# Expert stage: the first half of the next expert's rows is transposed ahead of the second half of gate and up

## The chip, the cores and the metric

One core of one Trainium2 chip runs the whole program. The metric is the device time of one execution in microseconds (us). Before the change it is 2176.31 us, the median of 3 runs (2172.53 to 2176.81).

The core's engines work side by side and meet at semaphores: TensorE (PE, and PEld for its weight loads), VectorE (DVE), ScalarE (ACT), GpSimd (POOL), which here issues the indirect transfers and small copies, and SyncE (SP), which issues the other transfers. Each engine runs its own instructions in the order in which they are written.

## The reference, cut to what matters

One layer of a decoder over 2048 prompt tokens and 64 sample tokens: a mixer (attention beside a short convolution), then 64 routed experts, of which each token uses 6, and one shared expert. The change lies in the routed experts:

```python
def step(acc, blk):
    tok, g, e = blk
    xb = xpad[tok]                                        # rows of the block's tokens, 1024 wide
    hid = jax.nn.silu(xb @ w_gate[e]) * (xb @ w_up[e])    # 1024 -> 256, twice
    yb = (hid @ w_down[e]) * g[:, None]                   # 256 -> 1024
    return acc.at[tok].add(yb.astype(acc.dtype)), None
```

## The kernel before

The program has four stages: mixer, dense part (output projection, norm, router, shared expert), routed experts (`stage_experts`, from about 1000 us of the span on), and the last norm. Only the third is changed.

All products are made from two parts for precision: an operand is rounded to a high part (by ACT) and the rest is taken as the low part (by DVE). "Round" and "split" below are these two steps, for weights (`round_w`, L1707; `split_w`, L1804) and for rows (`round_x`, L1714; `split_x`, L1809).

An expert takes up to n rows: 256 for the first two, then 176, 192, 208, 224, 240 and 256 in six classes (`CLASSES`, L61) with 10, 14, 10, 12, 8 and 8 experts. Experts go in pairs p; b is the place in the pair, and expert e = 2p + b. Rows come as two halves t, of 128 and of n - 128 rows. What each engine does for an expert:

- POOL gathers the rows into `xg` (L1663), one indirect transfer for each half, and later adds the outputs into memory (L1646).
- PE transposes a half with 8 instructions of 128x128 into `psX` (L1867). There is one `psX`, so the second half must wait until ACT and DVE have read the first (`s_xl`, L1865).
- ACT rounds that half into `xs` (L1714), and DVE splits it (L1809). There is one `xs` (beyond the first pair), so the rounding of expert e's first half must wait until both halves of gate and up of expert e-1 are done (`s_gu`, L1713).
- PE computes gate and up in two halves f of 128 of the 256 hidden columns (`gate_up`, L1870): 32 matmuls each, in turn of 2n columns (L1881) and of n columns (L1883), into `psU`. When one f is done, ACT first copies its second part out (`copy_lo`, L1686), DVE adds (L1786), then come a sigmoid (L1691) and products.
- PE computes down of expert e-2, for each half t 12 matmuls of 512 columns into `psY` (L1859 to L1861), and ACT writes the scaled output (L1724).

In one step of PE, which this text numbers by the expert e whose rows are transposed, stand: gate and up of e-1 with f = 1, transpose of e's first half, down of e-2 for its first half, transpose of e's second half, down of e-2 for its second half, gate and up of e with f = 0. The order of ACT is written out by hand in its own `pair` (L1743) and that of DVE likewise (L1828): on ACT, `copy_lo(e-1, 1)` stands directly ahead of `round_x` of e's first half. The first pair (`fresh`) has another order. So 62 of the 64 experts, e = 2 to 63, have the step above.

The lines that make the waits named in the prediction:

```python
pe.wait_ge(s_row[2 * b + t], 16 * (p + 1))             # L1864: rows gathered
after(pe, s_xl, 2 * e + t - (1 if fresh(p) else 0))    # L1865: psX read by the split
act.wait_ge(s_xT, 2 * e + t + 1)                       # L1711: transposed
after(act, s_gu, 2 * e)                                # L1713: gate and up of e-1 done
```

Of the kernel before, what the change touches and what calls it, by code (L numbers as in the profile page):

```python
# [140 lines left out]
def after(eng, sem, count):  # L141


    if not (isinstance(count, int) and count <= 0):
        eng.wait_ge(sem, count)
# [1383 lines left out]
def stage_experts(nc, io, ov, raw, ent, s_ent, s_w, s_norm):  # L1529
    PAIRS = NE // 2  # L1530
    with ExitStack() as ctx:
# [48 lines left out]
        def pairs(eng, pair, peeled=1):  # L1580


            pair(0, BLK, BLK, None)
            more = eng.value_load(ov[0:1, MORE:MORE + 1], min_val=0, max_val=OVP)
            before = BLK
            for begin, end, n in CLASSES:
                for p in range(begin, begin + peeled):
                    pair(p, before, n, None)
                    before = n
                with eng.Fori(begin + peeled, end) as p:  # L1590
                    pair(p, n, n, None)
            with eng.If(more > 0):
                with eng.Fori(0, OVP) as j:
                    with eng.If(more > j):
                        pair(PAIRS + j, BLK, BLK, j)
            return PAIRS + more
# [257 lines left out]
        @block.tensor  # L1854
        def _(pe):
            pe.wait_ge(s_const, 16)

            def three(out, lh, ll, rh, rl, start, stop):
                nc.tensor.matmul(out, lh, rh, start=start, stop=False)  # L1859
                nc.tensor.matmul(out, lh, rl, start=False, stop=False)  # L1860
                return nc.tensor.matmul(out, ll, rh, start=False, stop=stop)  # L1861

            def transpose_x(p, e, b, t):
                pe.wait_ge(s_row[2 * b + t], 16 * (p + 1))  # L1864
                after(pe, s_xl, 2 * e + t - (1 if fresh(p) else 0))  # L1865
                for kc in range(KC):
                    last = nc.tensor.transpose(rows_T(p, t)[:, kc * P:(kc + 1) * P], xg[:, 2 * b + t, kc * P:(kc + 1) * P], ident[:])  # L1867
                last.then_inc(s_xT, 1)

            def gate_up(e, b, f, n):  # L1870
                if not exists(e):
                    return
                if f == 0:
                    pe.wait_ge(s_xl, 2 * e + 2)
                after(pe, s_sum, 2 * e + f - 1)
                for half in range(2):
                    c0 = half * FF + f * P
                    for kc in range(KC):
                        if f == 0 and half == 0 and kc % 2 == 0:
                            pe.wait_ge(s_split, 6 * e + kc // 2 + 1)  # L1880
                        nc.tensor.matmul(psU[:, f, half, 0:2 * n].rearrange("p (s n) -> p s n", s=2), guh[:, b, kc, c0:c0 + P],  # L1881
                                         rows_split(e)[:, kc, :, 0:n], start=(kc == 0), stop=False)
                        last = nc.tensor.matmul(psU[:, f, half, 0:n], gul[:, b, kc, c0:c0 + P], rows_split(e)[:, kc, 0, 0:n],  # L1883
                                                start=False, stop=(kc == KC - 1))
                last.then_inc(s_gu, 1)

            def down(e, b, t, n):
                if not exists(e):
                    return
                pe.wait_ge(s_hl, 2 * e + 2)  # L1890
                pe.wait_ge(s_split, 6 * e + 6)
                r = rows_of(n, t)
                for half in range(2):
                    u = 2 * t + half
                    after(pe, s_y, 4 * e + u - 1)
                    for f in range(FC):
                        last = three(psY[0:r, half, :], hdh[:, b, f, t * P:t * P + r], hdl[:, b, f, t * P:t * P + r],
                                     dnh[:, b, f, half * 512:(half + 1) * 512], dnl[:, b, f, half * 512:(half + 1) * 512],
                                     f == 0, f == FC - 1)
                    last.then_inc(s_dn, 1)  # L1900

            def pair(p, n1, n, j):
                for b in range(2):
                    e = 2 * p + b
                    if not fresh(p):
                        gate_up(e - 1, 1 - b, 1, n if b else n1)
                    for t in range(2):
                        transpose_x(p, e, b, t)
                        down(e - 2, b, t, n1)
                    if fresh(p):  # L1910
                        gate_up(e - 1, 1 - b, 1, n)
                    gate_up(e, b, 0, n)

            e = 2 * pairs(pe, pair)
            for t in range(2):
                down(e - 2, 0, t, BLK)
            gate_up(e - 1, 1, 1, BLK)
            pe.wait_ge(s_split, 6 * e)
            pe.wait_ge(s_y, 4 * e - 4)
            pe.wait_ge(s_sum, 2 * e - 1)  # L1920
            for f in range(FC):
                pe.wait_ge(s_hl, 2 * e - 1 + f)
                for u in range(4):
                    t, half = u // 2, u % 2
                    last = three(last_sums(u), hdh[:, 1, f, t * P:(t + 1) * P], hdl[:, 1, f, t * P:(t + 1) * P],
                                 dnh[:, 1, f, half * 512:(half + 1) * 512], dnl[:, 1, f, half * 512:(half + 1) * 512],
                                 f == 0, f == FC - 1)
                    if f == FC - 1:
                        last.then_inc(s_dn, 1)
# [197 lines left out]
```

## Time and profile before

| | value |
|---|---|
| median of 3 runs | 2176.31 us (2172.53 to 2176.81) |
| the profiled execution | 2175.58 us, span 2173.8 us |
| PE busy | 2056.9 us, 95% of the span |
| DVE busy | 1429.4 us, 66% |
| ACT busy | 1208.0 us, 56% |
| POOL busy | 573.5 us, 26% |
| mean granted TensorE clock | 0.976 of full speed |
| memory traffic | read 316.91 MB, written 98.12 MB |

The profiled execution is 0.73 us shorter than the median of the runs. Its span is the time from the first to the last recorded instruction, and 1.8 us of the execution lie around it. A busy share is a mean over all stages. PE's matmuls overlap in the records: a matmul of 512 columns is recorded with 0.39 us, while the next one starts 0.23 us after it. So the distance from start to start tells what a matmul costs, not its recorded length.

### The profile page before, as it was taken

Reading aid. Unit: us, or ns where it says so; the run is one execution under the profiler, and the core shown is the slowest. Engines: PE = TensorE matmul, PEld = TensorE weight load, DVE = VectorE, ACT = ScalarE, POOL = GpSimd, SP = SyncE. Lnnn points to the kernel's source line nnn. Section 1 sums busy time; section 2 is a strip of 40 time slices with the busy share of each in tenths; the row PEclk is TensorE's granted clock in tenths of the full one; section 3 lists DMA queues with packets and bytes.
Section 4 is the critical chain, followed back from the end, with each engine's and each line's share of the span. In section 5 each row is a group of like instructions: output and inputs, shape, how many; then the busy total and the mean of one; then the engine's idle time right before and its main releaser. Section 6 shows DMA issues by size and latency. Waiting matters only on the chain. (4 is left out here: it accounts for less than half of the span.)

```text
span 2173.8 us, 36506 instructions
## 1 busy us (share of the span) xinstructions
PE 2056.9 (95%) x11572; PEld 1739.6 (80%) x11572; DVE 1429.4 (66%) x2742; ACT 1208.0 (56%) x2133; POOL 573.5 (26%) x659
## 2 busy tenths in 40 slices
PE   7999999999899999986999999999999999999970
PEld 5787777777678888875988889989988888888860
DVE  6444454444668787876777777777777777777738
ACT  5343443443533333323777777777777777767648
POOL 1111111111112323233233333333333333333320
PEclk9999999999999999998999999999999999999985
DMA  6111011010453223246799999999999999999957
GB/s 213 49 42 38 30 37 44 30 36 34 164 202 102 92 93 101 83 172 217 223 307 271 293 297 277 293 299 283 277 290 293 292 293 286 290 287 286 285 111 302
DMA packets 113290, 413.81 MB, mean 190 GB/s; under 512 B 35185, under 2 KB 39793, under 8 KB 85521
## 3 DMA queue, kind: packets, MB, share of 16 engines
q1 hardware_dynamic: 75344, 290.02, 36.1%
q0 software_dynamic: 37872, 122.90, 25.1%
q8 instruction: 36, 0.59, 0.1%
q14 instruction: 38, 0.30, 0.0%
HBM read 316.91 MB, written 98.12 MB: 191 GB/s over the span
## 5 line engine op out<-in xcount | busy, mean ns | idle before, releaser
L1881 PE MATMUL ex_psU<-ex_xs,ex_guh 128*128 128x384 f32 (+5 forms) x2016 | 620.6, 371 | 2.4 <-DVE ex_xs L1809 2.4
L1883 PE MATMUL ex_psU<-ex_xs,ex_gul 128*128 128x192 f32 (+5 forms) x2016 | 523.0, 259 | 0.0
L1881 PEld LDWEIGHTS ex_psU<-ex_xs,ex_guh 128*128 128x128 f32 x2016 | 378.6, 188 | 34.3 <-DVE ex_xs L1809 2.6
L1883 PEld LDWEIGHTS ex_psU<-ex_xs,ex_gul 128*128 128x128 f32 x2016 | 384.4, 191 | 2.5
L1646 POOL DMA_INDIRECT acc_d<-ex_y,ex_rows x128 | 198.9, 1554 | 397.4 <-ACT ex_y L1724 380.7
L1663 POOL DMA_INDIRECT ex_xg<-h_d,entries x128 | 143.8, 1124 | 345.7 <-issue 214.9
L1859 PE MATMUL ex_psY<-ex_dnh,ex_hdh 128*128 128x512 f32 x508 | 209.6, 413 | 1.9 <-DVE ex_hdl L1798 1.0
L1861 PE MATMUL ex_psY<-ex_dnh,ex_hdl 128*128 128x512 f32 x508 | 200.0, 394 | 0.0
L1860 PE MATMUL ex_psY<-ex_dnl,ex_hdh 128*128 128x512 f32 x508 | 199.0, 392 | 0.0
L1724 ACT ACTIVATE ex_y<-ex_psY,ex_use 128x512 f32<-128x512 f32 x254 | 169.4, 681 | 27.5 <-PE ex_psY L1861 27.1
L1786 DVE TENSOR_TENSOR ex_gu<-ex_psU,ex_lo 128x384 f32<-128x384 f32 (+5 forms) x128 | 77.3, 604 | 151.3 <-ACT ex_lo L1686 150.0
L1809 DVE TENSOR_TENSOR ex_xs<-ex_psX,ex_xs 128x512 fp32r<-128x512 f32 (+5 forms) x125 | 130.7, 1046 | 61.7 <-ACT ex_xs L1714 56.7
L717 PE MATMUL mi_psG<-mi_gh,mi_xh 128*128 128x512 f32 x408 | 168.7, 414 | 0.9 <-DVE mi_gl L539 0.9
L1804 DVE TENSOR_TENSOR ex_gul<-mi_g_raw,ex_guh 128x1024 fp32r<-128x1024 f32 x128 | 155.9, 1220 | 10.1 <-ACT ex_guh L1707 10.1
L1804 DVE TENSOR_TENSOR ex_gul<-mi_g_place,ex_guh 128x1024 fp32r<-128x1024 f32 x128 | 155.9, 1220 | 8.5 <-ACT ex_guh L1707 8.5
L717 PE MATMUL mi_psG<-mi_gl,mi_xh 128*128 128x512 f32 x408 | 160.4, 393 | 0.0
L717 PE MATMUL mi_psG<-mi_gh,mi_xl 128*128 128x512 f32 x408 | 160.4, 393 | 0.0
L1686 ACT ACTIVATE ex_lo<-ex_psU 128x384 f32<-128x384 f32 (+5 forms) x128 | 67.1, 524 | 159.1 <-PE ex_psU L1883 158.1
L1707 ACT ACTIVATE ex_guh<-mi_g_raw 128x1024 fp32r<-128x1024 f32 x128 | 134.1, 1050 | 11.2 <-PEq L895 11.2
L1867 PE MATMUL ex_psX<-ex_ident,ex_xg 128*128 128x128 f32 x1008 | 131.4, 273 | 7.0 <-DMA ex_xg<-h_d,entries 7.0
L1707 ACT ACTIVATE ex_guh<-mi_g_place 128x1024 fp32r<-128x1024 f32 x128 | 134.0, 1050 | 0.0
L1867 PEld LDWEIGHTS ex_psX<-ex_ident,ex_xg 128*128 128x128 f32 x1008 | 115.9, 141 | 16.1 <-issue 7.1
(398 smaller groups left out, 4180.8 us busy)
## 6 DMA issues: line engine op xcount, KB each, us to landing
mi_g_raw<-w_experts SPq DMA_DIRECT2D x96, 1024.0 KB
mi_g_place<-w_experts SPq DMA_DIRECT2D x96, 1024.0 KB
mi_xr<-xT SPq DMA_DIRECT2D x17, 512.0 KB, 3.7
acc_d<-de_acc SPq DMA_DIRECT2D x17, 512.0 KB, 13.3
h_d<-de_h POOLq DMA_DIRECT2D x17, 512.0 KB
de_cr<-cat SPq DMA_DIRECT2D x16, 512.0 KB
de_xr<-x_rows SPq DMA_DIRECT2D x16, 512.0 KB
mi_g_raw<-w_conv SPq DMA_DIRECT2D x6, 1024.0 KB, 20.9
```

Source lines behind the costliest of these rows:

```text
L717: last = nc.tensor.matmul(psG[:, (k + j) % 2, :], a[:, k, kc, :], b[:, j, kc, :], start=(kc == 0 and n == 0), stop=(kc == KC - 1 and n == 2))
L1646: nc.gpsimd.indirect_dma_start(out=io["acc_d"], out_offset=bass.IndirectOffsetOnAxis(ap=rows[0:r, 2 * b + t:2 * b + t + 1].bitcast(U32), a ...
L1663: nc.gpsimd.indirect_dma_start(out=xg[0:r, k, :], out_offset=None, in_=io["h_d"], in_offset=bass.IndirectOffsetOnAxis(ap=ent[0:r, k, 0:1]. ...
L1707: A(hi, src, ACT.Copy).then_inc(s_round, 1)
L1724: A(y[0:r, k, half * 512:(half + 1) * 512], sums(u)[0:r], ACT.Copy, scale=use[0:r, k, 1:2].bitcast(F32)).then_inc(s_y, 1)
L1804: V.tensor_tensor(lo, src, hi.bitcast(F32), ALU.subtract).then_inc(s_split, 1)
L1859: nc.tensor.matmul(out, lh, rh, start=start, stop=False)
L1860: nc.tensor.matmul(out, lh, rl, start=False, stop=False)
L1861: return nc.tensor.matmul(out, ll, rh, start=False, stop=stop)
L1867: last = nc.tensor.transpose(rows_T(p, t)[:, kc * P:(kc + 1) * P], xg[:, 2 * b + t, kc * P:(kc + 1) * P], ident[:])
L1881: nc.tensor.matmul(psU[:, f, half, 0:2 * n].rearrange("p (s n) -> p s n", s=2), guh[:, b, kc, c0:c0 + P], rows_split(e)[:, kc, :, 0:n], st ...
L1883: last = nc.tensor.matmul(psU[:, f, half, 0:n], gul[:, b, kc, c0:c0 + P], rows_split(e)[:, kc, 0, 0:n], start=False, stop=(kc == KC - 1))
```

## The change

In the pair of PE, the transpose of the first half (t = 0) is issued ahead of gate and up of e-1 with f = 1, where it stood behind it. The second half's transpose keeps its place between the two parts of down. In the first pair nothing moves, since gate and up is not issued there ahead of the transposes. No instruction of another engine is moved.

```diff
             def pair(p, n1, n, j):
                 for b in range(2):
                     e = 2 * p + b
+                    transpose_x(p, e, b, 0)
                     if not fresh(p):
                         gate_up(e - 1, 1 - b, 1, n if b else n1)
-                    for t in range(2):
-                        transpose_x(p, e, b, t)
-                        down(e - 2, b, t, n1)
+                    down(e - 2, b, 0, n1)
+                    transpose_x(p, e, b, 1)
+                    down(e - 2, b, 1, n1)
                     if fresh(p):
                         gate_up(e - 1, 1 - b, 1, n)
                     gate_up(e, b, 0, n)
```

On PE, between gate and up of expert 2 with f = 0 (176 rows) and the same with f = 1, in the step of expert 3 (`ex_xg` holds the gathered rows, `ex_psX` their transpose, `ex_rows2` says that the first half has been gathered, `ex_xT_lo` that the rows before have been split):

```order
 L1881 MATMUL ex_psU<-ex_xs,ex_guh 128x352
 L1883 MATMUL ex_psU<-ex_xs,ex_gul 128x176
+L1867 MATMUL ex_psX<-ex_ident,ex_xg 128x128 [waits ex_xT_lo,ex_rows2]
+L1867 MATMUL ex_psX<-ex_ident,ex_xg 128x128 x7
 L1881 MATMUL ex_psU<-ex_xs,ex_guh 128x352 [waits ex_summed]
 L1883 MATMUL ex_psU<-ex_xs,ex_gul 128x176
```

The eight transposes of the first half, with their two waits, now stand between the halves of gate and up.

On PE, at the end of the second half of gate and up in the same step, 32 matmuls later, where down of expert 1 begins:

```order
 L1881 MATMUL ex_psU<-ex_xs,ex_guh 128x352
 L1883 MATMUL ex_psU<-ex_xs,ex_gul 128x176
-L1867 MATMUL ex_psX<-ex_ident,ex_xg 128x128 [waits ex_xT_lo,ex_rows2]
-L1867 MATMUL ex_psX<-ex_ident,ex_xg 128x128 x7
 L1859 MATMUL ex_psY<-ex_dnh,ex_hdh 128x512 [waits ex_y,ex_split,ex_hid_lo]
 L1860 MATMUL ex_psY<-ex_dnl,ex_hdh 128x512
```

Down follows gate and up directly, and between the end of gate and up and the transpose of the second half only the 12 matmuls of down are left.

On ACT, in a step of the class of 192 rows, in both kernels alike (`ex_lo` is the target of `copy_lo`, `ex_xs` the rounded rows):

```order
L1686 ACTIVATE ex_lo<-ex_psU 128x2x192 [waits ex_hid,ex_gate_up]
L1714 ACTIVATE ex_xs<-ex_psX 128x8x128 [waits ex_gate_up,ex_xT]
L1691 ACTIVATE ex_lo<-ex_gu 128x192 [waits ex_summed]
L1707 ACTIVATE ex_guh<-mi_g_place 128x1024 [waits gate_up_back_loaded1]
L1724 ACTIVATE ex_y<-ex_psY,ex_use 128x512 [waits ex_added,ex_entries_kept,ex_down]
```

The copy of `psU` stands ahead of the rounding of the first half, and both wait for gate and up; nothing here is moved.

## Rows read from the trace of the kernel before

**Rows 1.** Stretches: time, busy us (count) by engine, clock, DMA share, GB/s.

```profile
1000.00:1030.00 30.00, 21.13 (x114) 18.47 (x114) 22.04 (x24) 17.84 (x22) 11.31 (x11) 0.78 0.85 289
1500.00:1600.00 100.00, 100.00 (x619) 90.95 (x618) 72.11 (x96) 72.10 (x107) 33.09 (x36) 1.00 0.97 287
```

**Rows 2.** Timeline of PE, one step of 208 rows: start us, length us, instruction.

```profile
1501.18 0.35 PE L1881 MATMUL ex_psU<-ex_xs,ex_guh 128*128 128x416 f32 x1
...
1510.66 0.26 PE L1883 MATMUL ex_psU<-ex_xs,ex_gul 128*128 128x208 f32 x1
1510.76 1.03 PE L1867 MATMUL ex_psX<-ex_ident,ex_xg 128*128 128x128 f32 x8
1511.55 0.47 PE L1859 MATMUL ex_psY<-ex_dnh,ex_hdh 128*128 128x512 f32 x1
1511.86 0.40 PE L1860 MATMUL ex_psY<-ex_dnl,ex_hdh 128*128 128x512 f32 x1
...
1514.17 0.40 PE L1861 MATMUL ex_psY<-ex_dnh,ex_hdl 128*128 128x512 f32 x1
1514.41 1.04 PE L1867 MATMUL ex_psX<-ex_ident,ex_xg 128*128 128x128 f32 x8
...
1518.08 0.35 PE L1881 MATMUL ex_psU<-ex_xs,ex_guh 128*128 128x416 f32 x1
```

**Rows 3.** Timeline of ACT in the same step.

```profile
1510.96 0.52 ACT L1686 ACTIVATE ex_lo<-ex_psU 128x416 f32<-128x416 f32 x1
1511.83 1.03 ACT L1714 ACTIVATE ex_xs<-ex_psX 128x1024 fp32r<-128x1024 f32 x1 [0.36 <-issue]
...
1515.48 0.71 ACT L1714 ACTIVATE ex_xs<-ex_psX 128x640 fp32r<-128x640 f32 x1 [0.18 <-PE ex_psX L1867]
```

**Rows 4.** Timeline of DVE in the same step.

```profile
1512.89 1.23 DVE L1809 TENSOR_TENSOR ex_xs<-ex_psX,ex_xs 128x1024 fp32r<-128x1024 f32 x1 [0.79 <-ACT ex_xs L1714]
...
1516.22 0.82 DVE L1809 TENSOR_TENSOR ex_xs<-ex_psX,ex_xs 128x640 fp32r<-128x640 f32 x1 [0.23 <-ACT ex_xs L1714]
```

**Rows 5.** Timeline of PE's weight loads: second half's transposes, same step.

```profile
1514.17 1.03 PEld L1867 LDWEIGHTS ex_psX<-ex_ident,ex_xg 128*128 128x128 f32 x8
```

**Rows 6.** Timelines of PEld and PE: such a load in a later step.

```profile
1598.73 0.96 PEld L1867 LDWEIGHTS ex_psX<-ex_ident,ex_xg 128*128 128x128 f32 x8
1598.90 1.03 PE L1867 MATMUL ex_psX<-ex_ident,ex_xg 128*128 128x128 f32 x8
```

**Rows 7.** Timeline of ACT: the copy, with 256 rows its follower, with 176 alone.

```profile
2032.29 0.60 ACT L1686 ACTIVATE ex_lo<-ex_psU 128x512 f32<-128x512 f32 x1 [3.04 <-PE ex_psU L1883]
2032.79 1.05 ACT L1707 ACTIVATE ex_guh<-mi_g_place 128x1024 fp32r<-128x1024 f32 x1
...
1161.36 0.47 ACT L1686 ACTIVATE ex_lo<-ex_psU 128x352 f32<-128x352 f32 x1 [1.72 <-PE ex_psU L1883]
```

**Rows 8.** Timelines of DVE and PEld in the first expert: a released wait.

```profile
1011.13 1.23 DVE L1809 TENSOR_TENSOR ex_xs<-ex_psY,ex_xs 128x1024 fp32r<-128x1024 f32 x1 [0.84 <-ACT ex_xs L1714]
1012.41 0.19 PEld L1881 LDWEIGHTS ex_psU<-ex_xs,ex_guh 128*128 128x128 f32 x1 [2.61 <-DVE ex_xs L1809]
1012.52 0.19 PEld L1883 LDWEIGHTS ex_psU<-ex_xs,ex_gul 128*128 128x128 f32 x1
```

**Rows 9.** Timeline of PE in the first pair: gate and up behind a transpose.

```profile
1021.36 0.48 PE L1881 MATMUL ex_psU<-ex_xs,ex_guh 128*128 128x512 f32 x1
1021.67 0.28 PE L1883 MATMUL ex_psU<-ex_xs,ex_gul 128*128 128x256 f32 x1
```

**Rows 10.** Timeline of POOL: two gathers for the next expert and an add.

```profile
1510.79 1.15 POOL L1663 DMA_INDIRECT ex_xg<-h_d,entries  x1 [5.26 <-issue]
1512.25 0.93 POOL L1663 DMA_INDIRECT ex_xg<-h_d,entries  x1 [0.30 <-issue]
...
1516.15 1.60 POOL L1646 DMA_INDIRECT acc_d<-ex_y,ex_rows  x1 [2.78 <-ACT ex_y L1724]
```

**Rows 11.** POOL's DMA queue from 1515 to 1520 us: packets, MB, share.

```profile
q0 software_dynamic: 236, 0.87, 57.7%
```

## The prediction

> **What bounds the kernel now.** I read the table of stretches first. In the routed experts PE is recorded busy for all of 100 us, at the full clock of 2.4 GHz (granted 1.00), while DVE and ACT are busy for 72 us each [rows 1]. Only the first 30 us of the stage are different (PE 21.13 us busy, clock 0.78). Since a recorded busy PE can hide small gaps, I then read PE's timeline of one step, from start to start. Gate and up of two halves takes 1510.76 - 1501.18 = 9.58 us, 4.79 us a half. The first half's transposes run from 1510.76; the second matmul of down starts at 1511.86, and from there to the last at 1514.17 are ten matmuls, 0.231 us each. The second half's transposes follow at 1514.41, 0.24 us behind the last matmul of down, which is the same distance as between matmuls of down. So PE has no gap at all [rows 2]. A step costs what PE's instructions cost, and 62 steps stand in a row. Whatever PE waits in a step is added to the time 62 times, and only a wait of PE that exists today could be won.
>
> Next I followed what releases the second half's transposes, because that wait is close. The chain runs over three engines. Gate and up ends at 1510.66 + 0.26 = 1510.92. ACT starts its copy of `psU` at 1510.96, then idles 0.36 us until the transposes are done, and rounds from 1511.83 to 1512.86 [rows 3]. DVE splits from 1512.89 to 1514.12 [rows 4]. The weight load of the second half's first transpose starts at 1514.17 [rows 5], 0.05 us behind the split. The reader is to see that this chain ends just in time: down's last matmul also starts at 1514.17.
>
> **The change, part by part.** PE's instructions are the same in number and kind. The moved piece is eight transposes with two waits and their signal; it issues no DMA and no queue is passed.
>
> What it moves on PE: eight transposes take from 1510.76 to 1511.55 by their starts, and then one load lies bare, since the first two matmuls of down are 0.31 us apart instead of 0.23. That is 0.79 + 0.08 = 0.87 us [rows 2]. Ahead of gate and up they cost the same: where this order exists today, in the first pair, the first two matmuls are also 0.31 us apart [rows 9], with the same 512 columns. So on PE alone the move is worth nothing; I take 0, with 0.05 us a step to either side (3 us in all) for widths that the rows don't show behind a transpose.
>
> What it does to the chain: counted from the end of gate and up, down now starts 0.87 us earlier, and so the second half's transposes are due 0.87 us earlier. Does the rounding start as much earlier? Before, it started 1511.83 - 1510.92 = 0.91 us after gate and up, because it waited for the transposes, and the copy of `psU` lay hidden under them. Now the transposes are long done, but the copy still stands ahead of the rounding on ACT and can't start before gate and up has ended. The rounding starts 0.04 us + one copy after it. A copy costs ACT, from start to start, 0.50 us with 256 rows, that is its recorded 0.60 us less 0.10. With 176 rows it is recorded with 0.47 us, which gives about 0.37 [rows 7]; with 208 rows 0.52 - 0.10 = 0.42 [rows 3]. So the rounding moves up by 0.91 - 0.04 - 0.42 = 0.45 us where 0.87 is needed. Measured against down, the chain ends one copy later than today: 0.42 us with 208 rows.
>
> How much of this is covered? The load starts today 0.24 us ahead of its transpose (1514.17 and 1514.41). In a later step it starts only 1598.90 - 1598.73 = 0.17 us ahead, and nothing follows late, so at least 0.07 us is free [rows 6]. A load that has been released is followed by the next one 0.11 us later (1012.41 and 1012.52), which I take as the time that a bare load needs [rows 8]. So it can come 0.24 - 0.11 = 0.13 us later free of charge. The lower bound of the cover is 0, if 0.07 is luck of the recording; the upper one is 0.24 us, if only the transposes and not their loads waited. I take 0.13, the value nearest to a row.
>
> The sum: the copy by class is 0.37, 0.39, 0.42, 0.45, 0.47 and 0.50 us (evenly from 176 to 256 rows), for 10, 14, 10, 12, 8 and 8 experts: 3.7 + 5.5 + 4.2 + 5.4 + 3.8 + 4.0 = 26.6 us. Less 62 x 0.13 = 8.1 us this is 18.5 us of new waits of PE, 0.24 to 0.37 us each. With cover 0.24 it is 26.6 - 14.9 = 11.7 us, with none 26.6 us.
>
> The bound of 0.24 is also where a rule of the Trainium skill would lead ("TensorE: Matmul & The Clock Gate", Part 2, the step on LDWEIGHTS): PE pulls a weight load ahead of matmuls in flight. By it the loads would be in the array when the wait ends, and the sum would be 11.7 us. The rows show the load itself starting 0.05 us behind the split, both here and in the first expert [rows 4, 5, 8], so I keep 18.5 us.
>
> What is late next: behind PE's new wait, down of the second half, gate and up of the next expert and everything after shift with it, so no second wait arises there. On ACT the second half's rounding idles 0.18 us today for its transposes [rows 3]; ACT falls behind PE by the covered 0.13 us only, so 0.05 us is left. DVE's second split idles 0.23 us [rows 4]. With the full cover of 0.24 us these would cost some hundredths back. ACT's other work gets 0.87 us more ahead of the end of gate and up and 0.87 less behind it, where it idles over 1.7 us before the next copy [rows 7].
>
> What the earlier transposes take away from the gather: the next expert's first transposes would start at 1518.08 + 4.79 = 1522.87 instead of 1527.66. The gathers are issued at 1510.79 and 1512.25 [rows 10]. From 1515 to 1520 POOL's queue moves 0.87 MB [rows 11]; the two gathers are 208 rows of 4 KB, 0.85 MB, and the add behind them is issued only at 1516.15. If the queue is in order, both halves are there by 1520, and the first one, 0.52 MB, sooner: some 3 us to spare. I take 0; not hidden it is a rival below.
>
> **The sum against its own time.** The profiled execution took 2175.58 us (span 2173.8 and 1.8 around it), so 2194.1 us. The median of the runs is 0.73 us above it, which gives 2194.8. I predict 2194.5 us.
>
> **Rivals.**
> - *The chain isn't what PE waits for, and the kernel gets a little faster.* If ACT got through the copy sooner, or if today's transposes are themselves held back by the split, the shorter distance wins something. Place: PE at L1867 of the second half. It decides at a copy of 0.13 us or less, or a cover above 0.42. Price: at most the 0.05 us a step taken above for the seams, 62 x 0.05 = 3 us, so 2172.5 us. Against it: all rows of copies are 0.47 us or longer. With a cover between the two it ends within 4 us of before, about 2178.
> - *The gather comes late.* If the adds share the queue's turns with the gathers, a first half may land only when the burst ends, 2 us behind 1522.87 in my step. For it: DMA is busy at 0.97 [rows 1]. Price: 1 us in a step gives 62 us, 2256 us. Against it: the order and the 3 us to spare.
> - *The clock falls.* Each step now has a gap of PE. In the first 30 us of the stage, with PE 21.13 us busy, the granted clock was 0.78 [rows 1], that is for part of the time at the lower level of 1.2 GHz. Were it 0.97 over 1050 us, this would add 1050 x 0.03 = 32 us: 2226 us. Against it: there PE idled for 9 us of 30, here for 0.3 of 17. The Trainium skill has a rule that speaks for this rival ("TensorE: Matmul & The Clock Gate", "A second HAM failure mode: psum-queue depth-cycling"): frequent short idles between groups of matmuls make the clock swing. No row of this stage shows short idles, so the trace can't settle it; the 0.78 belongs to long ones.
>
> **How the numbers follow.** The forecast gets 0.84, the kernel ending faster 0.04, the cover that is large enough for no change 0.05, the gather 0.03, the clock 0.04. The bounds 11.7 and 26.6 us, with 3 us for the seams at either end, go from 2184 to 2206; the outer ends need both extremes, so the range is 2185 to 2204. What lies outside is mainly the rivals, 0.16. What can be told from no change here is 0.2%, 4.4 us: faster 0.04, same 0.05, slower 0.91.
>
> **What would show it.** In the profile after, PE's waits have a new line, `psX` on DVE's split (L1809), about 62 times with 0.2 to 0.4 us, or, where the profile counts it as busy, the distance from down's last matmul to the second half's transposes grows from 0.24 to about 0.5 us. The step of 208 rows grows from 16.90 by 0.29 us. ACT's copy is followed by the rounding with no idle time between. If the copy and the rounding follow each other and the distance stays at 0.24, the cover was mis-sized. A line of PE waiting for the gather, or a clock below 1.00 between 1100 and 2000 us, would show a rival. If the step is no longer than 16.90 us, the prediction is wrong.

## The result and the profile after

The changed kernel takes 2190.66 us, the median of 4 runs (2187.11 to 2191.82); the kernel before took 2176.56 us beside it (4 runs, 2172.53 to 2177.27). The ratio is 1.0067 with a 95% interval of 1.0055 to 1.0078: slower by 14.1 us. A second set of runs (below) gave 1.0077 [1.0063, 1.0091]. The forecast was 2194.5 us with 2185 to 2204. The profiled execution took 2187.11 us, with a span of 2185.3. One execution each in experiments 2, 8 and 9, and one of the kernel before beside 8 and 9, took 2322 to 7534 us, and the ratios leave these out.

First the page: the busy time of each engine over the span.

```profile
PE 2069.8 (95%) x11572; PEld 1737.7 (80%) x11572; DVE 1428.3 (65%) x2742; ACT 1200.3 (55%) x2133; POOL 576.7 (26%) x659
```

DVE's and ACT's work has not grown, but PE is recorded 12.9 us busier (2056.9 before) with the same instructions. The new time is hidden in PE's busy records.

PE's waits in the expert stage (engine, tile and line, what was waited for: us in total, times, longest us):

```profile
PE ex_psX L1867 <- DMA ex_xg<-h_d,entries: 7.1, 1, 7.1
...
PE ex_psX L1867 <- DVE ex_xs L1809: 0.9, 5, 0.2
```

The second line is new. It has 5 waits and 0.9 us, far below the whole loss, because a matmul that is still recorded as busy covers most of each wait. The first, the gather, is there once, as it was before; no step of the changed order waits for rows.

The row of the weight loads (PEld) shows what PE's row hides. Its waits for these transposes from 1020 to 2100 us:

```profile
PEld ex_psX L1867 <- DVE ex_xs L1809: 22.3, 50, 0.6
PEld ex_psX L1867 <- issue: 6.2, 12, 0.6
```

In the kernel before, neither line is there. So the load now waits in 62 places, which is the number of steps, and for 50 of them the split is named as what released it. The 28.5 us are idle time of the load row, not the loss: part of them is covered by matmuls that still run.

The stretches of [rows 1], with one more near the end of the stage (time, busy us and count by engine PE, PEld, DVE, ACT, POOL, then clock, DMA share, GB/s):

```profile
1000.00:1030.00 30.00, 25.12 (x137) 22.01 (x138) 20.75 (x24) 16.18 (x22) 9.76 (x10) 0.84 0.89 323
1500.00:1600.00 100.00, 100.00 (x614) 89.47 (x614) 71.40 (x94) 69.56 (x105) 33.43 (x34) 1.00 0.94 282
1900.00:2000.00 100.00, 99.30 (x563) 84.61 (x562) 70.45 (x88) 69.06 (x101) 33.75 (x34) 1.00 0.94 291
```

From 1500 to 1600 us PE is still 100.00 us busy, at the full clock, with 614 matmuls where 619 stood. The reader is to see that the busy time tells nothing here and that the count and the start-to-start distances do.

The timeline of PE in the same step of 208 rows, which answers to [rows 2] (start us, length us, instruction):

```profile
1503.77 0.35 PE L1881 MATMUL ex_psU<-ex_xs,ex_guh 128*128 128x416 f32 x1
...
1508.46 0.26 PE L1883 MATMUL ex_psU<-ex_xs,ex_gul 128*128 128x208 f32 x1
1508.56 1.03 PE L1867 MATMUL ex_psX<-ex_ident,ex_xg 128*128 128x128 f32 x8
...
1514.12 0.26 PE L1883 MATMUL ex_psU<-ex_xs,ex_gul 128*128 128x208 f32 x1
1514.21 0.42 PE L1859 MATMUL ex_psY<-ex_dnh,ex_hdh 128*128 128x512 f32 x1
1514.47 0.40 PE L1860 MATMUL ex_psY<-ex_dnl,ex_hdh 128*128 128x512 f32 x1
...
1516.78 0.39 PE L1861 MATMUL ex_psY<-ex_dnh,ex_hdl 128*128 128x512 f32 x1
1517.16 1.09 PE L1867 MATMUL ex_psX<-ex_ident,ex_xg 128*128 128x128 f32 x8
1518.01 0.48 PE L1859 MATMUL ex_psY<-ex_dnh,ex_hdh 128*80 128x512 f32 x1
...
1520.88 0.35 PE L1881 MATMUL ex_psU<-ex_xs,ex_guh 128*128 128x416 f32 x1
```

The step is 1520.88 - 1503.77 = 17.11 us, where it was 16.90. The first half's transposes stand in the middle of gate and up. Down's last matmul starts at 1516.78, and the second half's transposes 0.38 us later; it was 0.24. The block that follows takes 1518.01 - 1517.16 = 0.85 us, where the first half's took 0.79 [rows 2]: a released transpose is recorded from the start of its load. Together 0.14 + 0.06 = 0.20 us, which is the growth of the step (0.21).

Its weight load, which answers to [rows 5], and on ACT and DVE the chain that releases it, which answers to [rows 3, 4] (a number in brackets is idle time ahead of the instruction, and what ended it):

```profile
1517.16 0.86 PEld L1867 LDWEIGHTS ex_psX<-ex_ident,ex_xg 128*128 128x128 f32 x8 [0.41 <-DVE ex_xs L1809]
```

```profile
1514.41 0.52 ACT L1686 ACTIVATE ex_lo<-ex_psU 128x416 f32<-128x416 f32 x1 [0.84 <-PE ex_psU L1883]
1514.83 1.02 ACT L1714 ACTIVATE ex_xs<-ex_psX 128x1024 fp32r<-128x1024 f32 x1
...
1518.29 0.71 ACT L1714 ACTIVATE ex_xs<-ex_psX 128x640 fp32r<-128x640 f32 x1
```

```profile
1515.88 1.23 DVE L1809 TENSOR_TENSOR ex_xs<-ex_psX,ex_xs 128x1024 fp32r<-128x1024 f32 x1 [0.32 <-ACT ex_xs L1714]
```

Gate and up ends at 1514.12 + 0.26 = 1514.38. The copy starts at 1514.41, the rounding 0.42 us behind it without any idle time, the split at 1515.88, and it ends at 1517.11; the load starts 0.05 us later. The chain is 2.73 us long (3.20 before), 0.47 us shorter, but the second half's transposes come 0.85 us sooner behind gate and up. So it is now 0.38 us late against down.

The same in all six classes, as medians over their steps, each step compared with the same step before. "Late" is how much later against down's last matmul the split ends than before. "Cover" is what PE did not pay of it, that is, late less the growth of the distance from down's last matmul to the start of down's second half:

| rows | step before | after | growth | late | cover |
|---|---|---|---|---|---|
| 176 | 15.93 | 16.13 | 0.20 | 0.33 | 0.175 |
| 192 | 16.35 | 16.54 | 0.19 | 0.375 | 0.155 |
| 208 | 16.90 | 17.11 | 0.21 | 0.37 | 0.17 |
| 224 | 17.31 | 17.57 | 0.26 | 0.44 | 0.175 |
| 240 | 17.755 | 18.04 | 0.285 | 0.44 | 0.16 |
| 256 | 18.425 | 18.835 | 0.41 | 0.49 | 0.155 |

With 10, 14, 10, 12, 8 and 8 steps the growth sums to 15.4 us (the runs: 14.1 and 15.2). The spans of the two profiled executions differ by only 11.5 us, because in that of the changed kernel the stages ahead of the experts ended 3.6 us sooner.

### The profile page after: what moved, and what is told of

Its sections match the earlier page's. It is cut to its first block and busy times, and to the rows that moved or that the text cites. A ratio compares the mean times of both kernels' runs of the same rounds, so it can differ in the third digit from the quotient of the medians.

```text
span 2185.3 us, 36506 instructions
## 1 busy us (share of the span) xinstructions
PE 2069.8 (95%) x11572; PEld 1737.7 (80%) x11572; DVE 1428.3 (65%) x2742; ACT 1200.3 (55%) x2133; POOL 576.7 (26%) x659
## 5 line engine op out<-in xcount | busy, mean ns | idle before, releaser
L1881 PE MATMUL ex_psU<-ex_xs,ex_guh 128*128 128x384 f32 (+5 forms) x2016 | 628.9, 373 | 2.4 <-DVE ex_xs L1809 2.4
L1724 ACT ACTIVATE ex_y<-ex_psY,ex_use 128x512 f32<-128x512 f32 x254 | 166.4, 685 | 27.4 <-PE ex_psY L1861 26.9
L1867 PEld LDWEIGHTS ex_psX<-ex_ident,ex_xg 128*128 128x128 f32 x1008 | 111.0, 142 | 36.5 <-DVE ex_xs L1809 22.3
```

Of the source, the lines that this page charges most:

```text
L1724: A(y[0:r, k, half * 512:(half + 1) * 512], sums(u)[0:r], ACT.Copy, scale=use[0:r, k, 1:2].bitcast(F32)).then_inc(s_y, 1)
```

## Experiments

The theory: the second half's transposes wait for the chain copy of `psU`, rounding, split, which starts at the end of gate and up in whatever place the first half's transposes stand. Rivals: the moved transposes cost PE time at their new seams; a gap comes from the clock or the gather; the load could be pulled ahead, so that the wait is not real. Each ratio is against runs of the kernel before on the same chip.

**1. The changed kernel with the copy behind the rounding.** If the copy is the cause, the new order should cost nothing once it no longer stands ahead of the rounding. On DVE the split likewise goes ahead of the sums.

```diff
 # ACT
-                    copy_lo(e - 1, 1, m)
                     round_x(p, e, 0, n)
+                    copy_lo(e - 1, 1, m)
...
 # DVE
-                    sums(e - 1, 1, m)
                     split_x(p, e, 0, n)
+                    sums(e - 1, 1, m)
...
```

The lines left out here move the later steps of the same half back too: on ACT the sigmoid goes behind the second half's rounding, on DVE the products (`activate`) go behind the second half's split and one more of weights.

> The changed kernel, and on ACT the rounding of the next expert's first half stands ahead of the copy of psU (f = 1), on DVE its split ahead of the sum; sigmoid and what follows it move behind the second half's rounding and split. PE is as in the changed kernel. Theory A (the copy of psU is what keeps the second half's transposes waiting): the rounding starts 0.04 us after gate and up, the split is done 2.32 us after it, the load of the second half's transposes is due about 2.5 us after it, so no wait: 0 to 3 us above the kernel before, PE's distance from down's last matmul to the transposes back at 0.24 us. Theory B (the transposes between the two halves of gate and up cost PE time by themselves, by bare loads, waits or the loop's head): 12 to 16 us above the kernel before, as the changed kernel.

Measured: 2175.56 us (2171.8 to 2177.31) against 2175.69; ratio 1.0000 [0.9991, 1.0009]. The steps are 15.915, 16.33, 16.89, 17.30, 17.755 and 18.40 us, those of the kernel before. Timelines of PE, of its loads, of ACT and of DVE in this kernel:

```profile
1506.32 1.03 PE L1868 MATMUL ex_psX<-ex_ident,ex_xg 128*128 128x128 f32 x8
...
1511.98 0.42 PE L1860 MATMUL ex_psY<-ex_dnh,ex_hdh 128*128 128x512 f32 x1
...
1514.55 0.39 PE L1862 MATMUL ex_psY<-ex_dnh,ex_hdl 128*128 128x512 f32 x1
1514.78 1.03 PE L1868 MATMUL ex_psX<-ex_ident,ex_xg 128*128 128x128 f32 x8
```

```profile
1514.57 1.00 PEld L1868 LDWEIGHTS ex_psX<-ex_ident,ex_xg 128*128 128x128 f32 x8
```

```profile
1512.24 1.03 ACT L1714 ACTIVATE ex_xs<-ex_psX 128x1024 fp32r<-128x1024 f32 x1 [0.90 <-PE ex_psU L1884]
1513.16 0.51 ACT L1686 ACTIVATE ex_lo<-ex_psU 128x416 f32<-128x416 f32 x1
```

```profile
1513.30 1.22 DVE L1809 TENSOR_TENSOR ex_xs<-ex_psX,ex_xs 128x1024 fp32r<-128x1024 f32 x1 [1.90 <-ACT ex_xs L1714]
```

The rounding starts 0.10 us behind the end of gate and up, the split ends at 1514.52, and the load starts 0.05 us later, now 0.21 us ahead of its transpose. The transposes stand 0.23 us behind down, at the pitch of down's own matmuls. The whole loss goes with one copy, which decides for the theory. The edit also moves DVE's sum, but that was not in the chain: in the changed kernel DVE idles 0.32 us between the sum and the split, until the rounding is done. The order of PE is here that of the changed kernel, so the seams of the moved transposes cost nothing that can be measured, and nothing is won either: PE had no gap to lose.

**2. The kernel before with the same edit on ACT and DVE.**

> The kernel before with the same new order on ACT and DVE, to see what that order costs by itself. Both theories: PE has no wait in the kernel before, and none is made or won: within 3 us of it. Should it be slower, by a wait of PE for the second half's split ahead of gate and up, the same amount must be taken off the run beside it.

Measured: 2175.77 us, ratio 1.0001 [0.9991, 1.0010]. In the old order it does nothing, since the copy was hidden under the transposes. So experiment 1 did not cover a loss with some unrelated gain of the edit.

**3. The first half's transposes in the middle of the second half of gate and up.** They stand between gate's and up's 16 matmuls, nearer to their old place and 2.4 us later for the gather, but still ahead of the end of gate and up.

```diff
-            def gate_up(e, b, f, n):
+            def gate_up(e, b, f, n, between=None):
...
+                    if half == 1 and between is not None:
+                        between()
...
-                    transpose_x(p, e, b, 0)
...
-                        gate_up(e - 1, 1 - b, 1, n if b else n1)
+                        gate_up(e - 1, 1 - b, 1, n if b else n1, lambda: transpose_x(p, e, b, 0))
```

> The first half's transposes stand in the middle of gate and up with f = 1, between gate's 16 matmuls and up's 16. Theory A: what counts is only that they stand ahead of the end of gate and up, so the chain and the wait are the changed kernel's: 12 to 17 us above the kernel before. Theory B in the form that the place between the halves (a loop's head, a wait for the sum) is dear: that place is no longer used, 0 to 4 us. In the form of a bare load behind the transposes it predicts the changed kernel's time too, and only the run with the rounding first tells it apart.

Measured: 2189.73 us, ratio 1.0073 [1.0060, 1.0087], the loss of the change itself. PE's timeline:

```profile
1513.11 0.26 PE L1885 MATMUL ex_psU<-ex_xs,ex_gul 128*128 128x208 f32 x1
1513.21 1.04 PE L1867 MATMUL ex_psX<-ex_ident,ex_xg 128*128 128x128 f32 x8
1514.00 0.43 PE L1883 MATMUL ex_psU<-ex_xs,ex_guh 128*128 128x416 f32 x1
...
1519.04 0.39 PE L1861 MATMUL ex_psY<-ex_dnh,ex_hdl 128*128 128x512 f32 x1
1519.42 1.09 PE L1867 MATMUL ex_psX<-ex_ident,ex_xg 128*128 128x128 f32 x8
```

The distance of down to the second half's transposes is 0.38 us again. Of these two places neither is dearer than the other; both lie ahead of the end of gate and up, where the transposes no longer cover the copy.

**4. The changed kernel again**, unchanged, beside experiments 1 to 3.

> The changed kernel again, on the chip and in the rounds of the others, as their measure: 11 to 16 us above the kernel before.

Measured: 2190.85 us, ratio 1.0077 [1.0063, 1.0091]; its 176-row step is 16.11 us. The four sit on one chip with one set of runs of the kernel before, so the difference between 1 and 4 (15.3 us) is the price of the place of the copy.

**5 and 6. A further copy behind the copy of `psU`, in the changed kernel and in the kernel before.** It reads a weight tile into a buffer that nobody reads, so it adds only time on ACT. If ACT's time between the end of gate and up and the rounding is what is paid, it costs 62 times its distance in the changed kernel, and nothing where the transposes cover it.

```diff
                     copy_lo(e - 1, 1, m)
+                    if exists(e - 1):
+                        A(spare[:], guh[:, b, 0, 0:P].bitcast(F32), ACT.Copy)
```

> The changed kernel with one more instruction on ACT in each step, between the copy of psU and the rounding of the first half: a copy of 128x128 that nobody reads. By the copies' lengths (0.36 us with 352 columns, 0.50 us with 512, from start to start) it should take ACT 0.15 to 0.2 us. Theory A: the wait of PE grows by all of it, 62 x 0.18 = 11 us more than the changed kernel, 22 to 28 us above the kernel before. Theory B: ACT is not what PE waits for, as in the changed kernel, 12 to 16 us.

> The kernel before with the same extra copy. Both theories: ACT idles 0.19 to 0.36 us at this place for the transposes, and the cover of the load adds 0.13 us, so it is hidden: within 3 us of the kernel before. If this one grew by 11 us as well, the extra copy would cost time in another way than by the wait that theory A names.

Measured: 2199.59 us, ratio 1.0130 [1.0113, 1.0146], for the changed kernel, and 2171.78 us, ratio 1.0000 [0.9991, 1.0010], for the kernel before (2172.22 us beside both). Timelines of ACT and then PE in the changed kernel with the further copy:

```profile
1519.56 0.52 ACT L1687 ACTIVATE ex_lo<-ex_psU 128x416 f32<-128x416 f32 x1 [0.84 <-PE ex_psU L1886]
1519.98 0.30 ACT L1758 ACTIVATE ex_spare<-ex_guh 128x128 bf16<-128x128 f32 x1
1520.18 1.02 ACT L1715 ACTIVATE ex_xs<-ex_psX 128x1024 fp32r<-128x1024 f32 x1
```

```profile
1522.51 1.09 PE L1870 MATMUL ex_psX<-ex_ident,ex_xg 128*128 128x128 f32 x8 [0.19 <-DVE ex_xs L1812]
```

ACT in the kernel before with the further copy:

```profile
1506.39 0.52 ACT L1687 ACTIVATE ex_lo<-ex_psU 128x416 f32<-128x416 f32 x1
1506.80 0.30 ACT L1758 ACTIVATE ex_spare<-ex_guh 128x128 bf16<-128x128 f32 x1
1507.26 1.03 ACT L1715 ACTIVATE ex_xs<-ex_psX 128x1024 fp32r<-128x1024 f32 x1 [0.16 <-PE ex_psX L1870]
```

The further copy is recorded with 0.30 us, but it delays the rounding by 1520.18 - 1519.98 = 0.20 us. Every class's step is 0.20 us longer than in the changed kernel, and 62 x 0.20 = 12.4 us; the runs say 27.4 us in all, some 12 to 13 above the change alone. Once the cover is spent, a delay on ACT is paid in full. In the kernel before the rounding still idles 0.16 us for its transposes, and the copy costs nothing.

**7. The first half's transposes a whole half of gate and up earlier, for the second expert of each pair.** This takes the gather's margin away on purpose. They go ahead of gate and up of the expert before with f = 0, 4.8 us sooner still.

```diff
-                    transpose_x(p, e, b, 0)
+                    if fresh(p) or b == 0:
+                        transpose_x(p, e, b, 0)
...
+                    if not fresh(p) and b == 0:
+                        transpose_x(p, e + 1, 1, 0)
                     gate_up(e, b, 0, n)
```

> The changed kernel, and for every second expert the first half's transposes go up one more half of gate and up, 4.8 us earlier (ahead of f = 0 of the expert before). The wait for the copy is untouched, so theory A gives the changed kernel's 12 to 16 us, if the rows are there. This measures the margin of the gather: in the kernel before the first half's rows seem to have landed at 1518.5 to 1520 us, and these transposes would start at about 1518. So PE should now wait for the gather, 0.4 to 2 us in 31 steps: 12 to 60 us more. A rival says that the gather is done much earlier than its queue's bytes tell: then nothing is added.

Measured: 2258.28 us, ratio 1.0405 [1.0387, 1.0422], 86 us slower. PE's waits in the expert stage of this kernel, then POOL and PE in one pair, then stretches (the last two lie behind two single waits, of 2.01 and of 2.00 us):

```profile
PE ex_psX L1867 <- DMA ex_xg<-h_d,entries: 56.4, 29, 6.9
```

```profile
1537.30 1.03 POOL L1663 DMA_INDIRECT ex_xg<-h_d,entries  x1 [5.15 <-issue]
```

```profile
1547.10 1.39 PE L1867 MATMUL ex_psX<-ex_ident,ex_xg 128*128 128x128 f32 x8 [2.01 <-DMA ex_xg<-h_d,entries]
```

```profile
1400.00:1500.00 100.00, 94.91 (x579) 84.53 (x578) 63.64 (x87) 62.29 (x95) 31.87 (x32) 0.97 0.85 247
1547.00:1551.00 4.00, 3.90 (x18) 3.82 (x19) 1.66 (x2) 0.70 (x1) 1.67 (x2) 0.59 0.80 118
1436.00:1440.00 4.00, 3.27 (x25) 3.28 (x26) 2.30 (x2) 1.34 (x2) 1.66 (x2) 1.00 0.88 147
```

PE waits 2.01 us for rows whose gather was issued 1547.10 - 1537.30 = 9.8 us before. Carried over to the step of the prediction, with the gather issued at 1510.79 [rows 10], the first half would land at about 1520.6, and the changed order wants it at 1522.87: an estimated margin of 2.3 us. It differs from gather to gather. Over all gathers of both halves, this trace gives 4.2 to 11.7 us from issue to landing, with a median of 9.1, and 11.7 us would leave 0.4 us. The edit moved the need 4.8 us forward, 2.5 us beyond the estimated margin. Of the 29 waits one, of 6.9 us, is the first expert's and is there in the kernel before too. The other 28 sum to 49.5 us, 1.8 us in the mean.

The starts in the trace account for the 86 us. The 31 distances from down's last matmul to the moved transposes are 54.3 us longer than 31 x 0.23 us, and the blocks of these transposes 4.2 us longer than 0.79 us each. The second half's transposes come later as in the changed kernel, 17.4 us. The rest is the clock: behind 8 of the 28 waits the 32 matmuls that follow take longer than the same ones elsewhere, 10.2 us in all, and the granted clock over the 4 to 5 us behind each of them was 0.57 to 0.68, so PE ran for most of that time at the lower of its two levels (1.2 GHz). Together this is 86.1 us. These 8 waits were 1.9 to 2.9 us long, but seven of the other 20 were as long (1.9 to 2.8 us), and behind those the clock stayed at 1.00.

**8. Two further copies in the kernel before**, in two separate steps (ACT drained between). With a delay X of ACT between the copy and the rounding, the old order should begin to pay once X outruns the transposes' shadow and the cover.

> The kernel before, PE's order untouched, with two copies of 128x128 that nobody reads, one behind the other with a drain between, between the copy of psU and the rounding. From start to start they should keep ACT some X = 0.5 us; X is read from the trace. Theory A with the cover c of the weight load: PE loses in each step what of copy + X exceeds 0.87 us + c, with the copies 0.36, 0.39, 0.41, 0.44, 0.47 and 0.49 us. For X = 0.5 this is 62 x 0.05 = 3 us if c were 0, and nothing if c is 0.13 or more: 0 to 1 us above the kernel before. Theory B says nothing of this kernel but no change.

Measured: 2178.74 us, ratio 1.0011 [1.0002, 1.0019], 2.4 us slower, where 0 to 1 was expected. X is 0.58 us here. In the classes of 208 and 224 rows the split ends 0.11 and 0.14 us later against down, and the steps are 16.89 and 17.30 us, as before: that much lateness is still free. PE's distances grow by 2.8 us in all, 2.1 of them in the classes of 176 and 192 rows. There ACT reaches the copy only 0.28 and 0.18 us behind the end of gate and up, where it does so 0.04 us behind it in the other classes. It does much the same in the kernel before (0.28 and 0.14 us), where the idle time ahead of the rounding absorbs it; the expectation did not count this. The size was missed, and the reading of the cover stands.

**9. Three further copies in the kernel before.**

> The same with three copies, X some 0.8 us: the chain from gate and up to the second half's transposes is then as late as in the changed kernel, with PE's order of before. Theory A: for X = 0.8, the excess of copy + X over 0.87 is 0.29 to 0.42 us, mean 0.35; with c = 0.17 (as the traces of before and after give) 11 us, with c = 0.13 14 us, with c = 0.24 7 us, with c = 0 22 us above the kernel before. Theory B (the place of the transposes costs by itself): no change, since PE's order is the old one.

Measured: 2202.59 us, ratio 1.0116 [1.0098, 1.0134], about 26 us slower, where 11 were expected. In this kernel the order of PE is the old one. PE, then ACT, then DVE:

```profile
1508.80 1.03 PE L1874 MATMUL ex_psX<-ex_ident,ex_xg 128*128 128x128 f32 x8
1509.59 0.48 PE L1866 MATMUL ex_psY<-ex_dnh,ex_hdh 128*128 128x512 f32 x1
...
1512.18 0.39 PE L1868 MATMUL ex_psY<-ex_dnh,ex_hdl 128*128 128x512 f32 x1
1512.70 1.09 PE L1874 MATMUL ex_psX<-ex_ident,ex_xg 128*128 128x128 f32 x8
```

```profile
1509.01 0.51 ACT L1687 ACTIVATE ex_lo<-ex_psU 128x416 f32<-128x416 f32 x1
1509.41 0.30 ACT L1758 ACTIVATE ex_spare<-ex_guh 128x128 bf16<-128x128 f32 x1
1509.78 0.31 ACT L1760 ACTIVATE ex_spare<-ex_guh 128x128 bf16<-128x128 f32 x1
1510.16 0.31 ACT L1762 ACTIVATE ex_spare<-ex_guh 128x128 bf16<-128x128 f32 x1
1510.38 1.01 ACT L1715 ACTIVATE ex_xs<-ex_psX 128x1024 fp32r<-128x1024 f32 x1
```

```profile
1511.42 1.22 DVE L1816 TENSOR_TENSOR ex_xs<-ex_psX,ex_xs 128x1024 fp32r<-128x1024 f32 x1 [1.28 <-ACT ex_xs L1715]
```

The expectation counted X = 0.8 us, but the copies delay the rounding by 1510.38 - 1509.41 = 0.97 us: a drained copy costs 0.37 us, not 0.30. With this X the expectation's own sum is 62 x (0.43 + 0.97 - 0.87 - 0.16) = 23 us. The other 2 to 3 us fit the classes of 176 and 192 rows, where ACT again reaches the copy 0.29 and 0.18 us behind gate and up. The split ends at 1512.64, 0.46 us behind the start of down's last matmul, where before it ended 0.05 us ahead of it: 0.51 us late. The distance to the transposes is 0.52 us, 0.28 more than before, and their block is 0.06 longer: 0.34 paid, 0.17 covered. Over the classes the cover is 0.18, 0.155, 0.18, 0.175, 0.16 and 0.155 us, a mean of 0.16, as in the changed kernel. So with PE's order untouched, lateness costs what it costs there. The distances from down's last matmul to down's second half grow by 25.4 us in all.

No experiment pointed to a version faster than the kernel before. PE has no wait in a step there, and what would be needed is less work on PE.

## Why the prediction was right, and where it was off

**What bounds the kernel.** Held. A step costs PE's instructions, 62 times, and experiments 1, 2 and 6 show that rearranging or adding work under it moves nothing.

**The move is worth nothing on PE itself** (taken as 0, with 3 us to either side). Held: 1.0000 [0.9991, 1.0009] with the moved order in experiment 1, a bound of 2 us.

**The chain ends one copy later against down.** The mechanism held, and every link of it is in the rows after. The size was somewhat too large. Forecast were 0.37 to 0.50 us by class; measured 0.33 to 0.49, 0.01 to 0.05 us less in each. For the step of 208 rows the terms are: the copy starts 0.03 us behind gate and up, not 0.04; the rounding is 0.01 us shorter (1.02 against 1.03); and down's last matmul comes 0.85 us earlier (3.25 us behind the end of gate and up before, 2.40 now), not 0.87, because its first two matmuls are still 0.26 us apart and not 0.23. Together 0.04. Over the 62 steps the lateness sums to 25.2 us, where 26.6 were forecast.

**The cover.** Taken as 0.13 us, measured 0.157 in the mean. The working took 0.24 us of lead less 0.11 us for a bare load. Both terms were off, in opposite directions. The released block of transposes takes 0.85 us instead of 0.79, so the bare load costs 0.06 us, not 0.11. The lead of the load in the kernel before is 0.14 to 0.24 us, with a mean of 0.21, so 0.24 was among its largest values. The lead less 0.06 us gives the measured cover of every class within 0.01. Over 62 steps the cover is 9.7 us, where 8.1 were taken. So 18.5 us becomes 25.2 - 9.7 = 15.5; the steps grew by 15.4 us. That 0.13 came so close is in part luck, since one error offset the other.

**The signs.** Of the two forms in which the wait was to show, PE's own line of waits did not come (5 of them, not about 62), and the distance did. In the step of 208 rows it is 0.38 us, where about 0.5 was written, and the step grew by 0.21 us, not 0.29: 0.04 less lateness and 0.04 more cover. The line that was looked for stands in the row of the weight loads, 62 times, where the prediction did not look.

**The 256-row class.** Its step grew by 0.41 us, its measured wait is 0.34. The remaining 0.07 us, some 0.6 us over 8 steps, lies in gate and up with f = 0. Its 32 matmuls take 5.70 to 5.74 us in five of the seven steps, where those of experiment 1 take 5.55 to 5.65; many are 0.01 us further apart and none of them waits. In the kernel before this class's steps scatter as well, from 18.38 to 18.62 us. The reason is left open.

**The rule on loads.** The Trainium skill ("TensorE: Matmul & The Clock Gate", Part 2, the step on LDWEIGHTS) lets PE pull a load ahead of matmuls in flight, which would have given 11.7 us. Here the load of a waiting transpose starts 0.05 us behind the split in each kernel looked at (1517.16 behind 1517.11, 1514.57 behind 1514.52), so it waits itself. Over all steps it is 0.04 to 0.12 us. The page says nothing of a wait that stands ahead of the pair; that a load would pass it was read into the rule, and these rows decide against it. They do not speak against the overlap itself: before, the load starts 0.24 us ahead of its transpose, beside down's last matmul.

**Rivals.** *Faster* is out: the lateness is above the cover in every class. The no-change case needed a cover above 0.3 us. *The clock*: 1.00 from 1100 to 2080 us. Gaps of 0.13 to 0.39 us once a step did not lower it, nor did those of 0.3 to 0.67 us in experiments 5 and 9, while some of 1.9 to 2.9 us in experiment 7 did. The Trainium skill's section "A second HAM failure mode: psum-queue depth-cycling" ("TensorE: Matmul & The Clock Gate") names frequent short idles as a danger without a length; this case shows no such effect at 0.67 us and below. *The gather*: never waited for after the first; but the margin was an estimated 2.3 us, not "some 3", less for the slowest gathers, and experiment 7 shows that its price is what was feared, 1.8 us in each of 28 steps.

**What is late next.** "Nothing" held: ACT's second rounding idled 0.18 us and has no idle time now, and PE's down of the second half follows at its pitch.

## What to carry to other kernels

Before moving an instruction ahead, follow the chain that it was covering: here a 0.42 us copy on ACT ran free in the shadow of eight transposes, and moving them uncovered it 62 times. Measure the distance between the two ends that race (the split and down's last matmul), not the idle time of PE, since 15 us of new waits left its busy share at 95% and 0.9 us of recorded waits. Ask for the waits of the weight loads as well: there all 62 showed. If such a move is wanted for another reason, the work that it uncovers goes behind the chain (experiment 1), and then the move is free.

## What the runs showed of the hardware that was not expected

- A weight load that stands behind a wait costs PE 0.06 us once it is released (blocks of 0.85 and 0.79 us), less than the 0.11 us between two bare loads of [rows 8].
- A small copy on ACT (128x128) is recorded with 0.30 us and costs 0.20 us between two others; with a drain behind it, 0.37 us from start to start.
- Gaps of PE of 0.13 to 0.67 us in each step (the changed kernel, experiments 5 and 9) leave the granted clock at 1.00. Of 28 waits of 0.2 to 2.9 us in experiment 7, 8 were followed by slower matmuls (granted clock 0.57 to 0.68 over 4 to 5 us) and 20 were not.
- An indirect gather of 128 rows of 4 KB landed 9.8 us after its issue beside the weights' transfers (DMA share 0.85), though its issue takes 1 us of POOL; over all gathers it was 4.2 to 11.7 us.
